# A hybrid decoder step on one core: one-hot gate blocks in every other group of u blocks, their gates stored in four parts, scatter heads of three tiles in rotation, the first u blocks split beside the q projections

## The reference

```
q = (t @ w_q), 8 heads, two halves of 64
s1, s2 = q halves against 128 sub keys each
v1, i1 = top_k(s1, 16); v2, i2 = top_k(s2, 16)
sc, ci = top_k(v1[:, None] + v2[None, :], 16)
e = i1[ci // 16] * 128 + i2[ci % 16];  gate = softmax(sc)
hid = u[e] . t                      # 128 picked rows of u per token
out = sum(gate * gelu(hid) * v[e])  # 128 picked rows of v per token
```

## Time and profile before

| | |
|---|---|
| median of 3 runs | 2143.62 us (2140.54 to 2146.57) |
| profiled execution | 2141.58 us, span 2139.8 us |
| TensorE, matmul busy | 2025.1 us, 95% of the span |
| VectorE busy | 1211.6 us, 57% |
| ScalarE busy | 621.8 us, 29% |
| GpSimd busy | 1125.8 us, 53% |
| mean granted TensorE clock | 0.967 of full speed |
| chain that ended last | TensorE 92%, VectorE 4%, DMA 2%, ScalarE 1% |
| its largest lines | u product (L795) 40%, v product (L889) 29%, first projections (L536) 9% |
| transfers | 365.24 MB, mean 171 GB/s |

### The profile page before, as it was taken

The page is one execution under the profiler, slowest core; times in us unless marked ns, Lnnn a source line. Parts: engine busy times, 40 slices in busy tenths (PEclk is TensorE's granted clock), DMA queues, the critical chain, the costliest instruction groups (busy, mean ns, idle before and its releaser), DMA issues.

```text
span 2139.8 us, 31840 instructions
## 1 busy us (share of the span) xinstructions
PE 2025.1 (95%) x12559; PEld 1858.2 (87%) x12559; DVE 1211.6 (57%) x2223; ACT 621.8 (29%) x971; POOL 1125.8 (53%) x697
## 2 busy tenths in 40 slices
PE   5999998699999999999998898999999999999996
PEld 3578777676889999999998898999999999999995
DVE  2325364733699787788343331112577777777774
ACT  2214112310332323232322322223333333333331
POOL 0023220200437778888788888774666666666300
PEclk8999998889999999999999998999999999999998
DMA  3097102022225555666555467657999999999961
GB/s 144 2 338 259 40 30 84 1 75 84 71 92 124 123 124 123 124 124 138 123 131 101 99 122 159 131 124 226 313 320 326 325 329 323 332 322 326 332 218 46
DMA packets 231733, 365.24 MB, mean 171 GB/s; under 512 B 92081, under 2 KB 157122, under 8 KB 230978
## 3 DMA queue, kind: packets, MB, share of 16 engines
q1 hardware_dynamic: 153282, 294.43, 41.3%
q0 software_dynamic: 78336, 69.25, 16.7%
HBM read 290.21 MB, written 73.38 MB: 170 GB/s over the span
## 4 chain that ended last, share of the span: by engine, by line
PE 92%; DVE 4%; DMA 2%; ACT 1%; issue 1%; POOL 0%; SPq 0%; DVEq 0%; ACTq 0%; POOLq 0%
PE bank L795 40%; PE bank L889 29%; PE bank L536 9%; PE bank L765 3%; PE bank L570 2%; PE bank L522 1%; DMA ring<-in_u 1%; PE bank L641 1%; DVE sq L1164 1%; PE bank L612 1%; DVE xn L1167 1%; PE bank L657 1%; PE bank L831 1%; PE bank L752 1%; PE bank L722 1%; PE bank L862 1%
## 5 line engine op out<-in xcount | busy, mean ns | idle before, releaser
L795 PE MATMUL bank<-xh,usp 128*128 128x288 f32 x4320 | 762.3, 298 | 32.5 <-DVE usp L1431 17.2
L1645 POOL DMA_INDIRECT gates_scratch<-gate_val,gate_at x384 | 666.1, 1735 | 159.3 <-issue 120.3
L795 PEld LDWEIGHTS bank<-xh,usp 128*128 128x128 f32 x4320 | 643.8, 191 | 35.1 <-DVE usp L1431 17.7
L889 PE MATMUL bank<-W,vsp 128*128 128x448 f32 x3072 | 622.8, 366 | 0.0
L889 PEld LDWEIGHTS bank<-W,vsp 128*128 128x128 f32 x3072 | 577.7, 188 | 44.8
L795 PE MATMUL bank<-xl,usp 128*128 128x288 f32 x2160 | 466.4, 298 | 0.0
L795 PEld LDWEIGHTS bank<-xl,usp 128*128 128x128 f32 x2160 | 352.2, 191 | 0.0
L1431 DVE TENSOR_TENSOR usp<-ring,usp 128x1024 fp32r<-128x1024 f32 x120 | 146.1, 1221 | 307.9 <-ACT usp L1062 307.6
L1539 DVE TENSOR_TENSOR vsp<-ring,vsp 128x1024 fp32r<-128x1024 f32 x128 | 156.9, 1226 | 169.0 <-ACT vsp L1127 169.0
L1069 ACT ACTIVATE gl<-bank 128x288 f32<-128x288 f32 x256 | 91.2, 409 | 553.3 <-PE bank L795 553.2
L1668 POOL DMA_INDIRECT picked<-in_v,row_index x128 | 149.7, 1169 | 184.7 <-DVE acc L1558 162.9
(11 more groups left out here) (245 smaller groups left out, 1588.8 us busy)
## 6 DMA issues: line engine op xcount, KB each, us to landing
ring<-in_u SPq DMA_DIRECT2D x128, 512.0 KB, 3.9
ring<-in_v SPq DMA_DIRECT2D x128, 512.0 KB, 5.2
hidden_scratch<-gl SPq DMA_DIRECT2D x128, 288.0 KB, 2.2
xn<-hidden_scratch SPq DMA_DIRECT2D x128, 224.0 KB, 5.9
G<-gates_scratch SPq DMA_DIRECT2D x120, 224.0 KB, 4.8
gates_scratch<-zero SPq DMA_DIRECT2D x32, 768.0 KB, 8.9
ring<-in_wproj SPq DMA_DIRECT2D x36, 512.0 KB, 3.5
gates_scratch<-gate_val,gate_at POOLq DMA_INDIRECT x384
```

The lines of the kernel that those rows point to most:

```text
L795: mm = pe.matmul(bank[b + y][:, 0:PHALF], w, src[:, k, y * PHALF:(y + 1) * PHALF], start=(k == 0 and w is hi and src is xh), stop=(k == KT ...
L889: mm = pe.matmul(bank[(k + 4) % 8][:, 0:TA], w, W[:, n % 4, z, :], start=(n == 0 and w is hi and z == 0), stop=(n == NE - 1 and w is lo))
L1645: pool.indirect_dma_start(gates_flat, bass.IndirectOffsetOnAxis(ap=gate_at[0:r, i, x:x + 1], axis=0), gate_val[0:r, i, hh, x - hh * TOPK:x ...
```

## The change

Four edits. `u_slot(n) = (n + 2) % 4` shifts the `usp` slot of block n by two, so that blocks 0 and 1 use slots 2 and 3; ScalarE makes their high halves during the last two q projections. The four gate blocks go into quads 20, 22, 24 and 26, and VectorE's splits are laid out anew around them. SP stores `stage` in four parts of 32 u blocks' rows each, behind quads 27, 28, 29 and 30. The scatter heads follow a list, `turns`, over three tiles.

```diff
+def u_slot(n):
+    return (n + 2) % NU
...
-            eng.wait_ge(gate_stored, 16)
+            eng.wait_ge(gate_stored, 16 * NBLK)
...  (SyncE)
-            with sp.Fori(POOL_SPLITS // 4, GATE_QUAD + NBLK) as q:
+            with sp.Fori(POOL_SPLITS // 4, GATE_QUAD + 2 * NBLK - 1) as q:
                 quad(q, False)
-            sp.wait_ge(gate_copied, NBLK * (TB // 4))
-            sp.dma_start(gates_dram[:, :, TS:TA].rearrange("n p t -> p n t"), stage[:, :, :]).then_inc(gate_stored, 16)
-            with sp.Fori(GATE_QUAD + NBLK, NE // 4 - 1) as q:
-                quad(q, False)
+            for b in range(NBLK):
+                quad(GATE_QUAD + 2 * NBLK - 1 + b, False)
+                part = slice(b * NE // NBLK, (b + 1) * NE // NBLK)
+                sp.wait_ge(gate_copied, NBLK * (TB // 4))
+                sp.dma_start(gates_dram[part, :, TS:TA].rearrange("n p t -> p n t"), stage[:, part, :]).then_inc(gate_stored, 16)
...  (TensorE; ScalarE alike)
             for b in range(NBLK):
-                quad(GATE_QUAD + b, False, gate=b)
-            with pe.Fori(GATE_QUAD + NBLK, NE // 4) as q:
+                quad(GATE_QUAD + 2 * b, False, gate=b)
+                quad(GATE_QUAD + 2 * b + 1, False)
+            with pe.Fori(GATE_QUAD + 2 * NBLK, NE // 4) as q:
                 quad(q, False)
...  (ScalarE, in the loop over the q projections)
+                if n >= N_PROJ - 2:
+                    split_u(n - (N_PROJ - 2), n - (N_PROJ - 2), 0)
                 from_pair(n, qh[:, n - N_FEAT - KT, :], half=PHALF)
...
-            for j in range(4):
+            for j in range(2, 4):
                 split_u(j, j, 0)
...  (VectorE)
             for b in range(NBLK):
-                own, n = slice(b * TB, (b + 1) * TB), 4 * (GATE_QUAD + b) - 4
+                own, n = slice(b * TB, (b + 1) * TB), 4 * (GATE_QUAD + 2 * b) - 4
+                split_u(n)
+                split_u(n + 1)
                 if b >= 1:
                     dve.wait_ge(one_hot_ready, b)
                 dve.tensor_tensor(hotA[:, :, :], index, bc(eT[:, 0, own], 2, NK), ALU.is_equal).then_inc(one_hot_step, 1)
-                for j in range(3):
-                    split_u(n + j)
+                split_u(n + 2)
                 if b >= 1:
                     dve.wait_ge(gate_done, b * (TB // 4))
                 dve.tensor_tensor(oneB[:, :, :], index, bc(eT[:, 1, own], 2, NK), ALU.is_equal)
+                split_u(n + 3)
                 dve.wait_ge(one_hot_step, b + 1)
                 for z in range(3):
                     ins = dve.tensor_tensor(oneA[:, z, :, :], hotA[:, :, :], bc(gparts[:, z, own], 2, NK), ALU.mult)
-                    if z == 0:
-                        split_u(n + 3)
+                    if z < 2:
+                        split_u(n + 4 + z)
                 ins.then_inc(one_hot_ready, 1)
-            for n in range(4 * (GATE_QUAD + NBLK) - 4, NE):
+                split_u(n + 6)
+                split_u(n + 7)
+            for n in range(4 * (GATE_QUAD + 2 * NBLK) - 4, NE):
                 split_u(n)
...  (GpSimd)
-            for i in range(TS // P + 1):
-                if i < TS // P:
+            turns = [0, 0, 0, 1, 0, 1, 2, 1, 2, 0, 2, 1, 2, 0, 2, 1, 0, 2, 1, 2, 0, 1, 2, 1]
+            heads = [0] * (TS // P)
+            for i in turns:
+                if heads[i] == 0:
                     pool.wait_ge(gates_ready, 2 * (i + 1))
-                for hh in range(PH // 2):
-                    if i >= 1:
-                        add_gates(i - 1, PH // 2 + hh)
-                    if i < TS // P:
-                        add_gates(i, hh)
+                add_gates(i, heads[i])
+                heads[i] += 1
```

More of the change, by code:

```diff
@@ L841, in quad @@
                         pe.wait_ge(gelu_ready, n - 1)
-                    mm = split_product(2 * (j % 2), j)
+                    mm = split_product(2 * (j % 2), u_slot(j))
                     mm.then_inc(hid_done, 1)
@@ L1040, in _, with split_u @@
             act.wait_ge(stored, MIXERS_STORED)
+            def split_u(n, j, round_):
+                act.wait_ge(ring_loaded[j], (round_ + (U_AT + 1)) * 16)
+                act.activation(usp[:, u_slot(j), 0, :], ring[:, j, :], ACT.Copy).then_inc(uhi_ready, 1)
             def copy_head(hh):
@@ L1057, in _ @@
                     copy_head(n - N_FEAT - KT - 2)
-            def split_u(n, j, round_):
-                act.wait_ge(ring_loaded[j], (round_ + (U_AT + 1)) * 16)
-                act.activation(usp[:, j, 0, :], ring[:, j, :], ACT.Copy).then_inc(uhi_ready, 1)
             def gelu(n, j, round_=None):
@@ L1118, in _ @@
             for b in range(NBLK):
-                quad(GATE_QUAD + b, gate=b)
-            with act.Fori(GATE_QUAD + NBLK, NE // 4 - 1) as q:
+                quad(GATE_QUAD + 2 * b, gate=b)
+                quad(GATE_QUAD + 2 * b + 1)
+            with act.Fori(GATE_QUAD + 2 * NBLK, NE // 4 - 1) as q:
                 quad(q)
@@ L1430, in split_u @@
                 dve.wait_ge(uhi_ready, n + 1)
-                dve.tensor_tensor(usp[:, n % NU, 1, :], ring[:, n % 4, :], usp[:, n % NU, 0, :].bitcast(F32), ALU.subtract
+                dve.tensor_tensor(usp[:, u_slot(n), 1, :], ring[:, n % 4, :], usp[:, u_slot(n), 0, :].bitcast(F32), ALU.subtract
                                   ).then_inc(ulo_ready, 1)
@@ L1633, in _ @@
                 pool.wait_ge(uhi_ready, n + 1)
-                pool.tensor_tensor(usp[:, n % NU, 1, :], ring[:, n % 4, :], usp[:, n % NU, 0, :].bitcast(F32), ALU.subtract
+                pool.tensor_tensor(usp[:, u_slot(n), 1, :], ring[:, n % 4, :], usp[:, u_slot(n), 0, :].bitcast(F32), ALU.subtract
                                    ).then_inc(ulo_first, 1)
```

## The result

Four executions of the changed kernel took 2123.44 us at the median (2110.65 to 2123.68), against 2142.08 before (2139.91 to 2146.57): ratio 0.9896, interval 0.9873 to 0.9919. The forecast was 2112 us, with a range of 2100 to 2125. Three of the four executions lie at 2123.4 to 2123.7, one at 2110.65; the profiled one is of the three.

What follows compares the result with a forecast made beforehand. Matmuls bound the kernel, with holes in the u product: 5.8 + 23.3 + 12.5 = 41.6 us. The scatter then sets the v product's start, leaving 31.2 net: 2112 us from a median of 2143.62, range 2100 to 2125.

Steps and rivals of the forecast that it cites:

- Which chain sets the end: Before the v product: scatter and gate loads set its start at 1453.3, 7.9 us after the u product's end.
- First u blocks: Beside the last q projections: early high halves start block 0 at about 600.2, gaining 5.8 us (bounds 3.9 and 5.85).
- One-hot blocks: Gate blocks in every other group of the u product: no waits between TensorE and VectorE, 23.3 us gained.
- Parts of the store: Gates stored in four parts: each lands in 5.7 to 7.2 us, TensorE waits for none, 12.5 us gained.
- Rival 3: Each store part holds SP's queue about as long as the whole did: 2152.0 us; chance 0.03.
- The scatter: GpSimd's scatter: two waits for heads, not nine, saving 22.2 us; start 1 us earlier, last instruction ends at 1438.1.
- From the last head to the loads: After the scatter: 2.1 us until the last head lands, eighth load issued 4.0 later, landing in 4.8.
- Slow clock behind the hole: Start of the v product: slow TensorE clock after the wait costs 2.5 us (bounds 1.5 and 3).
- The v product its 622.6 us: The v product keeps its duration of 622.6 us unchanged.
- Rival 1: The u product sets the end because the scatter ends over 8 us earlier: 2102.0 us; chance 0.13.
- rival C: Follow-up's rival: v pace settled by its start against feeding engines; 206.7 ns in most, 2121 us; no chance given.

Runs made afterwards that it cites:

- f1: Changed kernel with the old order of scatter heads, all else changed: 2136.44 us (2129.83 to 2147.33, ten executions).
- f5: Kernel before, with the new order of scatter heads only: ratio 0.9986 (0.9975 to 0.9998).
- f4: Changed kernel without the early split of u blocks 0 and 1 and the shifted slots: 2115.31, 2117.53, 2133.08, 2133.34 us; a fifth, 2263.19, left out.
- f2: Changed kernel with the one-hot blocks in four successive groups and VectorE's old order of work there: 2125.69 to 2143.03 us, ten executions.
- f3: Changed kernel with the gates stored by one DMA behind quad 27: 2110.44, 2113.11, 2116.49 and 2133.00 us.
- e2: Changed kernel with VectorE waiting for the first two gate loads alone: 2111.17 us (2106.44 to 2118.31).
- g2: Changed kernel with the last u block multiplied three times, twice into unused banks: 2110.89, 2111.94 and four at 2117.46 to 2118.62 us.
- g1: Changed kernel, VectorE waiting for the first two gate loads alone, store parts behind quads 26 to 29: 2104.68 us, ratio 0.9823.
- e4: Changed kernel with 36 float32 matmuls on TensorE between the last u block and the first v block: 2130.96 us (2127.38 to 2133.72).

## Why the prediction was right, and where it was off

- **Which chain sets the end.** Right: the gates do, and not the u product. The u product ended at 1444.7 (1445.4 said), then came 9.2 us of wait (7.9), and the v product started at 1453.87 (1453.3). f1 and f5 show it from both sides: the rotation is worth 17.3 us in the start of the v product here and about 0.1% of the time, some 3 us, in the kernel before. What the prediction did not have is that behind the rotation the transfers hold the gates, more than the scatter's own end.
- **First u blocks.** Block 0 started at 599.6 (600.2). The clock stayed at 1.00, so the higher bound of the slow clock was right: 5.8 said, 6.2 by f4. VectorE's split of block 9 held nothing up.
- **One-hot blocks.** No wait on either side; 23.3 said, 26.4 by f2, of which 2.2 is a gelu that waits for another reason.
- **Parts of the store.** A part lands in 7.0 us (5.7 to 7.2 said) and makes ScalarE at most 4.4 late (3.0 to 4.5). TensorE waits for none. 12.5 said, 11.5 by f3's u product. Rival 3 fell.
- **The scatter.** Its last instruction ended at 1430.9, 7.2 before 1438.1. The start was 3.3 us earlier than in the earlier trace rows and not 1, the waits took 5.6 and not 7.2, and the short stops that the old order had besides its nine waits (120.3 - 115.8) were gone. The time of its instructions stayed, as said: 667.4 us in sum against 666.1, and 667.4 to 674.9 in the traces with the rotation. That spread alone moves its end, to 1434.5 in e2 and 1435.1 in g2.
- **From the last head to the loads.** Mis-sized the other way: 6.9 us until it had landed (2.1 said) and 8.1 for the last load (4.8). I had held that the hidden loads would be mostly done. They were issued from 1420.9 on, right behind the last part of the store, and with the v loads they kept the transfers busy: the window 1430 to 1438 moves 310 GB/s at a share of 0.91. The two errors, 7.2 early and 8.1 late, nearly cancel. By the table under f4 that is only in part luck, since an earlier last instruction waits longer for the same transfers; that the forecast of the start came within 0.6 us is luck.
- **Slow clock behind the hole.** 2.5 said, about 2.
- **The v product its 622.6 us.** This is the term that failed: the prediction let it stand without a reason. It took 636.6 us in the profiled execution, 12.3 of the 14.0 by the pace of 206.7 ns, which 3 of 8 executions had. At the fast pace the kernel takes 2109.7 to 2116.1, and 2112 fits these. The median of the first four, 2123.44, lies in the range of 2100 to 2125 by luck: the top of the range was made up of late heads, long landings and waits for a part, and nothing in it stood for a second pace. Of the 31.6 us forecast, 18.6 came in that median.

Rival 1's case, that the u product sets the end, was made true by the edits of g1: 2102.0 said, 2104.68 measured (2099.6 to 2105.1).

**Left open:** what picks the pace. In the first trace of the changed kernel the matmuls from 1460 on all last 368 ns, right behind the slow clock, and it holds to the last of the 3072. The traces have the slow pace behind a hole of 9.2 us and of 27.6, behind a gap of 0.7 us, and behind 36 float32 matmuls with no gap (there in six of six); and the fast pace behind holes of 1.7, 4.4, 6.8, 8.4 and 9.1 us. Where u matmuls go straight over into v matmuls, the four traces (before, f5, g1, g2) are fast, and no execution of g1 or g2 is slow by its time. The chip alone does not decide: f1's ten executions, all on one chip, have both paces. That the instant of the v product's start against the engines that feed it decides, rival C of e4, was not tested by itself; no run moved that instant and nothing else. A cause is not shown.

## What to carry to other kernels

When holes are taken out of one chain, work out when the next one arrives, with its landings under the traffic of the new schedule and not of the old: here the u product ended 42 us sooner and the v product started 33 us sooner. Then look at what the waiting side really needs; two loads of eight, and a store one group earlier, gave back the rest. And test a part in both kernels: the rotation was worth about 0.1% in the old one and 17 us in the new. Before a difference of a few microseconds between two traces is put down to an edit, look how far two traces of the same kernel lie apart: here the scatter's instructions took 667.4 us in one and 671.1 in the other.

## What the runs showed of the hardware

- One instruction stream can run TensorE at two paces at the same granted clock of 1.00: 448-column matmuls 202.7 ns apart with durations of 361 to 370 ns, or 206.7 apart, all 368. Either holds over 3072 matmuls, and one program showed both. In this kernel that is a difference of 0.6% between two executions with no edit.
- A DMA of 4096 KB in rows of 256 B landed in 22.9 us, a quarter of it in 7.0. If the time is a fixed share and one that grows with the bytes, the fixed share is about (4 x 7.0 - 22.9) / 3 = 1.7 us, an estimate from these two sizes.
- The last indirect store of the scatter landed 2.0 us after its instruction in g1, with 152 GB/s moved meanwhile, and 2.1 us in f1, with next to nothing moved; it took 6.9 us in the changed kernel, where eight loads of 224 KB and two v loads had been issued in the 10 us before and 310 GB/s were moved.
